# Neighbourhood scores with two 128-row and two 64-row products per block in place of six 64-row ones

## The reference

```python
q = _rmsnorm(q.reshape(B, L, NA_HEADS, NA_HEAD_DIM), q_w)
k = _rmsnorm(k.reshape(B, L, NA_HEADS, NA_HEAD_DIM), k_w)
...
s_win = (jnp.einsum('bqhd,brqchd->bhqrc', q_row, k_win).astype(jnp.float32) * scale
         + bias.astype(jnp.float32)[None])
s_meta = jnp.einsum('bqhd,bmhd->bhqm', q_row, k_meta).astype(jnp.float32) * scale + meta_b
p = jax.nn.softmax(jnp.concatenate([s_win.reshape(...), s_meta], axis=-1), axis=-1)
```

## Time and profile before

| | us |
|---|---|
| median of 3 runs (1439.40 to 1441.11) | 1440.16 |
| the profiled execution, whole | 1438.17 |
| its span in the trace | 1436.4 |
| neighbourhood stage, first to last score | 1103.6 to 1380.3 |
| one pair in that stage | 36.5 |
| TensorE busy over the span | 1345.0 (94%) |
| VectorE busy | 776.6 (54%) |
| GpSimd busy | 605.8 (42%) |
| ScalarE busy | 512.7 (36%) |

### The profile page before, as it was taken

The page is one execution under the profiler, slowest core; times in us unless marked ns, Lnnn a source line. Parts: engine busy times, 40 slices in busy tenths (PEclk is TensorE's granted clock), DMA queues, the critical chain, the costliest instruction groups (busy, mean ns, idle before and its releaser), DMA issues.

```text
span 1436.4 us, 20233 instructions
## 1 busy us (share of the span) xinstructions
PE 1345.0 (94%) x6789; PEld 1080.8 (75%) x6789; DVE 776.6 (54%) x1514; ACT 512.7 (36%) x1080; POOL 605.8 (42%) x367
## 2 busy tenths in 40 slices
PE   4998999999999999999987799999989999999987
PEld 2776677777688888888866587877768888888866
DVE  3315666562655556531142477777534666666761
ACT  2322333411433334310022466666303444444420
POOL 3424233247244444455532344344254655555511
PEclk9999999999999999999998899999999999999999
DMA  5232222233132333233322111111133322222212
GB/s 153 74 74 77 62 66 74 59 89 103 59 102 88 102 88 98 88 110 93 97 76 69 30 45 30 44 39 34 31 101 100 85 67 64 65 68 69 59 30 73
DMA packets 196544, 105.38 MB, mean 73 GB/s; under 512 B 18974, under 2 KB 194428, under 8 KB 196492
## 3 DMA queue, kind: packets, MB, share of 16 engines
q1 hardware_dynamic: 195968, 103.98, 25.5%
q0 software_dynamic: 432, 0.69, 0.2%
q10 hardware_dynamic: 92, 0.02, 0.0%
HBM read 102.57 MB, written 2.10 MB: 73 GB/s over the span
## 4 chain that ended last, share of the span: by engine, by line
PE 79%; DVE 7%; issue 5%; POOL 3%; ACT 3%; DMA 1%; SPq 0%; DVEq 0%; POOLq 0%; ACTq 0%
PE ps L347 18%; PE ps L348 18%; PE ps L349 18%; PE ps L369 9%; PE ps L1192 1%; PE ps L1203 1%; POOL w_low L334 1%; PE ps L874 1%; DMA w_raw<-in_w_in_dram 1%; PE ps L1220 1%; PE ps L1222 1%; PE ps L1221 1%; POOL y_low L632 1%; PE ps L854 1%; DVE scaled L466 1%
## 5 line engine op out<-in xcount | busy, mean ns | idle before, releaser
L334 POOL TENSOR_TENSOR w_low<-w_raw,w_high 128x1024 fp32r<-128x1024 f32 x183 | 447.8, 2448 | 573.5 <-DVE w_high L329 573.4
L347 PE MATMUL ps<-h_high,w_high 128*128 128x512 f32 x864 | 354.8, 411 | 16.6 <-DVE h_low L470 11.7
L348 PE MATMUL ps<-h_low,w_high 128*128 128x512 f32 x864 | 343.9, 398 | 0.0
L349 PE MATMUL ps<-h_high,w_low 128*128 128x512 f32 x864 | 342.4, 396 | 0.0
L329 DVE CAST w_high<-w_raw 128x1024 fp32r<-128x1024 f32 x183 | 135.5, 742 | 152.7 <-PE ps L349 66.5
L347 PEld LDWEIGHTS ps<-h_high,w_high 128*128 128x128 f32 x864 | 164.0, 190 | 64.9 <-issue 21.2
L349 PEld LDWEIGHTS ps<-h_high,w_low 128*128 128x128 f32 x864 | 164.0, 190 | 37.8
L348 PEld LDWEIGHTS ps<-h_low,w_high 128*128 128x128 f32 x864 | 163.9, 190 | 35.5 <-issue 1.7
L1987 DVE SCALAR_TENSOR_TENSOR z<-ps,cv,z 128x511 f32<-128x511 f32 x44 | 33.0, 750 | 97.8 <-ACT z L1483 97.8
L1483 ACT ACTIVATE z<-ps,cv 128x512 f32<-128x512 f32 x44 | 34.3, 779 | 121.9 <-PE ps L349 121.7
L349 PE MATMUL ps<-m_high,w_low 128*128 128x512 f32 x176 | 69.4, 395 | 0.0
(11 more groups left out here) (326 smaller groups left out, 2527.6 us busy)
## 6 DMA issues: line engine op xcount, KB each, us to landing
w_raw<-in_w_in_dram SPq DMA_DIRECT2D x150, 256.0 KB, 3.2
w_raw<-in_w_up_dram SPq DMA_DIRECT2D x88, 256.0 KB, 3.1
w_raw<-in_w_out_dram SPq DMA_DIRECT2D x44, 256.0 KB, 3.0
w_raw<-in_w_down_dram SPq DMA_DIRECT2D x32, 256.0 KB, 3.0
w_raw<-in_w_down_dram SPq DMA_DIRECT2D x16, 192.0 KB, 2.6
rel<-in_rel_bias_dram SPq DMA_DIRECT2D x8, 384.0 KB, 3.2
x_tok<-in_x_dram SPq DMA_DIRECT2D x4, 512.0 KB, 5.9
w_raw<-in_w_ob_dram SPq DMA_DIRECT2D x8, 256.0 KB, 2.9
```

The costliest lines, as they stand in the source:

```text
L334: pool.tensor_tensor(w_low[:, n % RING, :], w_raw[:, n % RAW, :], w_high[:, n % RING, :].bitcast(F32), ALU.subtract).then_inc(low_made, 1)
L347: pe.matmul(acc, wh, mh, start=first and k == 0, stop=False)
L348: pe.matmul(acc, wh, ml, start=False, stop=False)
L349: done = pe.matmul(acc, wl, mh, start=False, stop=last and k == tiles - 1)
```

## The change

`scores` issues four products: for each head one over all 128 rows, and one over that head's own 64 rows. For the product over 128 rows the queries' high part and low part of one head are stacked (`nq_parts`: own half high, other half low), and the keys' high part of that head stands on both halves (`nk_twice`). The second product is the high queries by the low keys. The order is head 0's two, then head 1's two.

The parts are made in other places. ScalarE's `high_of` now works in two halves of 64 partitions for keys and for queries, so four activations in place of two. `root_exp` and the keys' `high_of` come before the exponentials of tile 3 and the queries' `high_of` right after these, both ahead of `keep_v`. VectorE gets `keys_twice` (two copies of 64 x 544, written to the other half of the partitions) between the queries' `normed` and `probs` of tile 3, and `rest_low` (three subtractions on 64 partitions: one of 544 columns, two of 512) between `probs` of tile 3 and `make_high`. GpSimd keeps one subtraction, 64 x 544, in place of two on 128 partitions. The scores of tile 0 wait for `n_parts`, which `rest_low` sets, and for `n_low`. The stacked queries lie in the last slice of `y_high` and `y_low`.

```diff
-                for q_, k_, one_, end in ((nq_high, nk_high, True, False), (nq_high, nk_low, False, False),
-                                          (nq_low, nk_high, False, True)):
-                    for h in range(2):
-                        d = slice(h * HD, (h + 1) * HD)
-                        mm = pe.matmul(ps[:, h, 0:w], q_[d, t * P:(t + 1) * P], k_[d, k0:k0 + w], start=one_, stop=end)
+                q = slice(t * P, (t + 1) * P)
+                for h in range(2):
+                    d = slice(h * HD, (h + 1) * HD)
+                    pe.matmul(ps[:, h, 0:w], nq_parts[h][:, q], nk_twice[:, h, k0:k0 + w], start=True, stop=False)
+                    mm = pe.matmul(ps[:, h, 0:w], nq_parts[h][d, q], nk_low[d, k0:k0 + w], start=False, stop=True)
...
-                dst, src = ((nk_high[:], nk_f[:]), (nq_high[:], nq_f))[m]
-                act.activation(dst, src, ACT.Copy).then_inc(s["n_high"], 1)
+                for h in range(2):
+                    d = slice(h * HD, (h + 1) * HD)
+                    dst, src = ((nk_twice[d, h, :], nk_f[d, :]), (nq_parts[h][d, :], nq_f[d, :]))[m]
+                    hi = act.activation(dst, src, ACT.Copy)
+                hi.then_inc(s["n_high"], 1)
...
-                expo(i, c, 3)
-                if more:
                     root_exp(i, c + 1, 1)
                     high_of(i, c + 1, 0)
+                expo(i, c, 3)
+                if more:
+                    high_of(i, c + 1, 1)
                     keep_v(i, c + 1)
-                    high_of(i, c + 1, 1)
...
+            def keys_twice(i, c):
+
+                dve.wait_ge(s["q_normed"], i * 6 + (3 * c + 2))
+                for h in range(2):
+                    own, other = slice(h * HD, (h + 1) * HD), slice((1 - h) * HD, (2 - h) * HD)
+                    dve.tensor_copy(nk_twice[other, h, :], nk_f[own, :])
+
+            def rest_low(i, c):
+                dve.wait_ge(s["n_high"], i * 4 + (2 * c + 1))
+                dve.tensor_tensor(nk_low[HD:P, :], nk_f[HD:P, :], nk_twice[HD:P, 1, :].bitcast(F32), ALU.subtract)
+                dve.wait_ge(s["n_high"], i * 4 + (2 * c + 2))
+                for h in range(2):
+                    own, other = slice(h * HD, (h + 1) * HD), slice((1 - h) * HD, (2 - h) * HD)
+                    lo = dve.tensor_tensor(nq_parts[h][other, :], nq_f[own, :], nq_parts[h][own, :].bitcast(F32),
+                                           ALU.subtract)
+                lo.then_inc(s["n_parts"], 1)
...
                 if more:
                     normed(i, c + 1, 1)
+                    keys_twice(i, c + 1)
                 probs(i, c, 3)
                 if more:
+                    rest_low(i, c + 1)
                     make_high(dve, ahead + 2, i * 8)
                     masked(i, c + 1, 0)
...
             normed(0, 0, 1)
+            keys_twice(0, 0)
             make_high(dve, N_NA + 5)
+            rest_low(0, 0)
             make_high(dve, N_NA + 6)
```

More of the change, by code:

```diff
@@ L183, in program @@
                 nk_f = sb("nk_f", [P, L + META], F32, a)
-                nk_high = sb("nk_high", [P, L + META], F32R, a)
+                nk_twice = sb("nk_twice", [P, 2, L + META], F32R, a)
                 nk_low = sb("nk_low", [P, L + META], F32R, a)
-                nq_high = sb("nq_high", [P, S], F32R, a)
-                nq_low = sb("nq_low", [P, S], F32R, a)
                 nv_high = sb("nv_high", [P, 2, 4, P], F32R, a)
@@ L201, in program @@
             nq_f, nvf = scaled[:, 0, 0:S], scaled[:, 1, :]
+            nq_parts = (y_high[:, 7, :], y_low[:, 7, :])
             with ExitStack() as a:
@@ L395, in program @@
             om_added rel_in nb_ready
-            q_sq q_kept q_sum q_root q_normed n_high n_low nv_kept nv_turned nv_high_ nv_low_ g_part g_done
+            q_sq q_kept q_sum q_root q_normed n_high n_low n_parts nv_kept nv_turned nv_high_ nv_low_ g_part g_done
             t_scored t_masked t_neg t_exp t_inv t_probs t_turned t_copied_a t_meta t_copied_b t_summed t_y
@@ L682, in bias_table, with low_of @@
                         .then_inc(s["nb_ready"], 1)
[L684 to L687, removed]
+            def low_of(i, c):
+                pool.wait_ge(s["n_high"], i * 4 + (2 * c + 1))
+                pool.tensor_tensor(nk_low[0:HD, :], nk_f[0:HD, :], nk_twice[0:HD, 0, :].bitcast(F32), ALU.subtract)\
+                    .then_inc(s["n_low"], 1)
             def y_parts(i, c):
@@ L704, in pair @@
                     make_low(pool, ahead + 1, i * 8)
-                    low_of(i, c + 1, 0)
-                    low_of(i, c + 1, 1)
+                    low_of(i, c + 1)
                     make_low(pool, ahead + 2, i * 8)
@@ L714, in _ @@
                 make_low(pool, n)
-            low_of(0, 0, 0)
-            low_of(0, 0, 1)
+            low_of(0, 0)
             for n in range(N_NA + 5, N_NA + 8):
@@ L1184, in scores @@
                 if t == 0:
-                    pe.wait_ge(s["n_low"], i * 4 + (2 * c + 2))
+                    pe.wait_ge(s["n_low"], i * 2 + (c + 1))
+                    pe.wait_ge(s["n_parts"], i * 2 + (c + 1))
                 if not first:
                     pe.wait_ge(s["t_masked"], i * 16 + (8 * c + 2 * t))
-                for q_, k_, one_, end in ((nq_high, nk_high, True, False), (nq_high, nk_low, False, False),
-                                          (nq_low, nk_high, False, True)):
-                    for h in range(2):
-                        d = slice(h * HD, (h + 1) * HD)
-                        mm = pe.matmul(ps[:, h, 0:w], q_[d, t * P:(t + 1) * P], k_[d, k0:k0 + w], start=one_, stop=end)
+                q = slice(t * P, (t + 1) * P)
[3 more added lines that the diff above has]
+                    mm = pe.matmul(ps[:, h, 0:w], nq_parts[h][d, q], nk_low[d, k0:k0 + w], start=False, stop=True)
                 mm.then_inc(s["t_scored"], 1)
@@ L1770, in pair @@
                     root_ln(i, c + 1, 1)
+                    root_exp(i, c + 1, 1)
+                    high_of(i, c + 1, 0)
                 expo(i, c, 3)
                 if more:
-                    root_exp(i, c + 1, 1)
-                    high_of(i, c + 1, 0)
+                    high_of(i, c + 1, 1)
                     keep_v(i, c + 1)
-                    high_of(i, c + 1, 1)
                 else:
@@ L2238, in keep @@
                 if c:
-                    dve.wait_ge(s["n_low"], i * 4 + (2 * c + m - 1))
+                    dve.wait_ge(s["n_parts"], i * 2 + c)
+                    dve.wait_ge(s["n_low"], i * 2 + c)
                 if m == 0:
```

## The result

The changed kernel takes 1478.8 us (median of 4 runs, 1474.35 to 1482.72) beside 1440.12 for the kernel before: ratio 1.0269, 95% interval [1.0253, 1.0285], 38.7 us more. The forecast was 1469.3 with a range that ended at 1477.0: the direction was right, the size 9.5 us too small, and the result lies outside the range. The profiled execution took 1477.01 with a span of 1475.3, so 38.9 more in the span.

The account below looks back on a forecast made before the run. The prediction took TensorE to bound the stage (busy 216.01 of 219 us) and summed 18.2 for its products, 7.0 for pair waits and 3.9 for the head to +29.1 us, median 1469.3. The range was 1454 to 1477.

Parts of the forecast that it names:

- TensorE's part: Score blocks on TensorE: four streams for three and four row-count changes for two, 0.54 or 0.60 us a block, 18.2 us.
- the fourth stream: Score block: the new products cannot run side by side, so four streams replace three, +0.12 us at 272 columns, +0.18 at 400.
- two more changes of row count: Score block: four changes between 128 and 64 rows in place of two, 0.21 us each, +0.42 us a block.
- Rival A: Score blocks: lone 64-row products load unseen, only the fourth stream is paid; +15.7 us, 1455.9; chance 0.12.
- rival D: Score blocks: the six products do not overlap, six streams become four, 9.6 us saved; 1430.6 with waits hidden; chance 0.05.
- The head: Start of the stage: first scores later because VectorE's and GpSimd's preparation take turns; +3.9 us, or +1.6 without GpSimd's strip.
- GpSimd's strip: Head of the stage: GpSimd's strip of 2.4 us gets in after the first of VectorE's three subtractions.
- The wait in each pair: Last quarter of a pair: tile 0's scores wait 1.0 us for n_parts, seven times, 7.0 us; bounds 0 to 14.
- the meeting: Pair's preparation: GpSimd's subtraction falls on VectorE's queries' normed, which would take 1.5 us and more; 0.75 alone.
- The first wait: End of a pair: keep_v is behind the queries' high_of, so turn_v waits some 0.4 of the 1.0 us.
- Rival C: Pair's preparation costs double, 2.0 us a pair; +36.1 us, 1476.3; chance 0.07.
- Rival B: TensorE pays in full, but VectorE and GpSimd do not meet and nothing new is waited for; +19.8 us, 1460.0; chance 0.13.

Follow-up runs that it names:

- four_on_old_parts: Kernel before with the changed kernel's product order (128 rows, 64, 128, 64) on the old parts, preparation unchanged: 1455.96 us, ratio 1.0111.
- six_full_rows: Kernel before with all six products of a block over all 128 rows, no change of row count: 1445.11 us, ratio 1.0037.
- halves_last: Kernel after with both 128-row products of a block first, then the two 64-row ones side by side: 1462.68 us, ratio 1.0163.
- no_pool_keys: Kernel after with GpSimd's subtraction of the keys cut from 544 to 16 columns in every pair but the first: 1469.85 us, ratio 1.0202.
- filled_wait: Kernel after with four overwritten 512-column products ahead of tile 0's scores in seven pairs, where TensorE waits for n_parts: 1476.82 us, ratio 1.0245.
- head_parts_first: Kernel after with rest_low ahead of make_high of a strip, at the head of the stage alone: 1475.78 us, ratio 1.0254.
- heads_apart: Kernel before with the two score loops exchanged, three products of head 0, then three of head 1: 1439.17 us, ratio 0.9997.

## Why the prediction was right in direction and too small

**TensorE's part: right.** Forecast 18.2, measured 17.3 in the kernel after (16 times 0.52 and 16 times 0.56) and 16.1 as the time of `four_on_old_parts`. The two terms it was made of, the fourth stream and two more changes of row count at 0.21, are each seen apart: the streams in `six_full_rows`, the changes in `halves_last` (0.52 per block back for one fewer stream and two fewer changes). Rival A (no price for the lone 64-row product) and rival D (six never overlapped) both fall, D by `six_full_rows` and by the result itself. The small error is in the rounding: 0.20, not 0.21, and the distances inside a block were 0.32 and 0.38 where 0.33 and 0.39 stood.

**The head: right.** Forecast 3.9, measured 4.1. GpSimd's strip did get in after the first subtraction, and the first subtraction of the queries took 2.73.

**The wait in each pair: right in kind, too small.** Forecast 1.0, measured 1.76; over seven pairs 5.3 us of the miss. The step that failed is the reckoning of both ends of that wait: the time at which `n_parts` is set and seen, and the time at which TensorE could have started.

Moved to the time of the pair shown above (55.65 us earlier than rows 5 to 8, by the row of L1203), the forecast had `normed` done at 1225.25 (measured 1225.14), the casts at 1225.95 (1226.06), `probs` at 1227.10 (1227.34) and `n_parts` at 1229.00 (1229.46). So the meeting was priced right, and the steps behind it too low. A cast takes 0.45 from start to start where 0.36 was taken, and a subtraction on 64 partitions 0.70 to 0.73 where 0.62 was taken; both were read off mean durations (427 and 708 ns) less 0.07 and 0.09 for an overlap. No such overlap exists between these instructions, as the starts in the rows show; the means as they stood would have been nearly right. `probs` took 1.26 where 1.14 was taken. Together that is 0.46 us a pair. Then TensorE started 0.24 us after the last subtraction, where 0.05 was taken: 0.19 more.

At the other end, the forecast moved the old start of the scores (1283.28), which lies behind the change to 64 rows: in rows 2 the first scores stand 0.31 behind the row of L1205. The new block begins with a product over 128 rows, which starts 0.14 behind that row when nothing is waited for (1219.47 to 1219.61). So TensorE was ready 0.17 earlier than the forecast had it, and waits as much longer. The three parts are 0.82 us, and the measured pairs are 0.76 longer than the forecast wait makes them.

The first wait, at L1251 for `nvf_meta`, came as forecast: 0.40 of idle time where some 0.4 stood, and `nvf_meta` was there at 1227.21, forecast 1227.15. It adds nothing to the pair, since the scores wait for VectorE's last subtraction all the same: in `no_pool_keys` it is gone, and the pairs are shorter by VectorE's 0.84 and no more.

**The clock: missed.** No term of the sum had it: 3.8 us in the profiled execution. The sum put it at nothing, without a reason. In the kernel after, TensorE waits 3.7 us before the first scores and 1.4 in each pair, and the granted clock fell to 1.2 GHz during the wait at the head and in two of the later pairs. It isn't the same in every execution: the mean clock of the four is 0.971 to 0.975, and the two slower ones have the lower values (1480.60 and 1482.72 us at 0.972 and 0.971). The times spread over 8 us, where the kernel before has 2 in 4 executions. `filled_wait` and `no_pool_keys` show the falls between pairs gone where the waits are filled or short. That the 2.14 us more in the first distance are the clock's is read from the profile (0.91 between 1100 and 1140) and was not tested apart. The forecast's own views had what was needed to raise the question: rows 1 have a clock of 1.00 at an idle share of 1.4%, and the forecast took that clock along while it forecast new waits.

**Ahead of the stage: most likely chance.** 1.4 us were there before any changed instruction ran. Profiled executions of the kernels built on the one after, which are the same up to there, lie further apart: the last projections after `root` start at 1100.65 in the kernel after, at 1099.11 in `head_parts_first` and at 1104.63 in `filled_wait`.

Together: 1.4 + 0.2 + 5.3 - 0.9 + 3.8 = 9.8, the difference between 38.9 and 29.1.

Rival C came nearest with its time, 1476.3, by a doubled wait of 2.0 per pair. As a mechanism it was wrong: the casts took 0.45 each and not 0.7, and GpSimd got in once and not twice. Rival B asked which of `normed` and GpSimd comes first. `halves_last` had it the other way round, and its reckoning (no gain) held. The range failed because its upper end was one rival's price for one term, with all others at their middle. The result lies 1.8 us past that end; the wait (5.3) and the clock (3.8) each account for more than that.

## What to carry to other kernels

Before products are merged, look whether the old ones shared the array: rows with the count "x2" and starts one stream apart are one stream, and merging them gains nothing. Count the changes between 64 and 128 rows as 0.2 us each; a block that has to mix both should keep equal row counts together, and padding with zeros to 128 rows can be cheaper than either (0.51 us for such a block, against 0.77 and 1.29). And when a forecast adds a wait to the engine that bounds the kernel, reckon both ends of the wait (here the engine also took 0.24 us to start after what it waited for), ask what the new idle time does to its clock, and take durations from start to start of the same shape.

## What the runs showed of the hardware

- Products on different row halves overlap though they are far apart in the instruction list (`heads_apart`: three of one head, then three of the other, started in twos at 1277.47, 1277.70 and 1277.83). The Trainium skill, "TensorEngine Tiling (Array Packing)", section Key Properties, says that separate tiles work in parallel, and the trace agrees, with the three starts just named. The time agrees too: 1439.17 beside 1439.86.
- Two changes of row count cost about as much as three more streams of 272 columns (0.40 against 0.36), and six 128-row products cost as much as six 64-row ones at 272 columns (0.75 against 0.77).
- A subtraction on 64 partitions takes what it takes on 128: on GpSimd 1.35 us for 64x544 and 1.39 for 128x544, on VectorE 0.72 for 64x544 and 0.708 for 128x528.
- When VectorE and GpSimd meet, either can be the one that is held: `normed` 1.59 in place of 0.75, GpSimd 1.77 in place of 1.35, casts 1.94 in place of 0.89.
- Waits of 1 us can be enough for TensorE's clock to fall: in the kernel after it went to 1.2 GHz in two of the later pairs, behind idle times of 0.4 and 1.0 us, and each of the two took 0.82 us more (41.22 in place of 40.40). Four pairs with the same waits kept 2.4 GHz.
